# The byte offsets of the feed-forward input and activation made the same in all stages

## What is computed

```python
def half_ffn(x, shift, scale, gate, g, w_gu, w_down):
    h = modulate(x, g, shift, scale)
    a, u = jnp.split(h @ w_gu, 2, axis=-1)
    return x + FFN_RES * gate * ((jax.nn.silu(a) * u) @ w_down)
...
    for i in range(DEPTH):
        xp = half_ffn(xp, mp[0], mp[1], mp[2], norm_ff1[i], ff1_w_gu[i], ff1_w_down[i])
...
        xp = half_ffn(xp, mp[6], mp[7], mp[8], norm_ff2[i], ff2_w_gu[i], ff2_w_down[i])
```

## Time and profile before

| | |
|---|---|
| median of 3 runs | 3004.07 us (3003.33 to 3004.99) |
| the profiled execution | 3003.66 us, of it 3001.8 us span |
| TensorE busy | 98% |
| VectorE busy | 76% |
| ScalarE busy | 42% |
| mean granted TensorE clock | 0.998 |

### The profile page before, as it was taken

The page is one execution under the profiler, slowest core; times in us unless marked ns, Lnnn a source line. Parts: engine busy times, 40 slices in busy tenths (PEclk is TensorE's granted clock), DMA queues, the critical chain, the costliest instruction groups (busy, mean ns, idle before and its releaser), DMA issues.

```text
span 3001.8 us, 44338 instructions
## 1 busy us (share of the span) xinstructions
PE 2932.3 (98%) x17575; PEld 2838.0 (95%) x17575; DVE 2288.0 (76%) x3506; ACT 1247.5 (42%) x2001; POOL 127.7 (4%) x135
## 2 busy tenths in 40 slices
PE   8999989999999998999999999999999999999999
PEld 6999879999999988999999987799999999889999
DVE  6889887888787877778788877678878887667553
ACT  3332464433333355443333247644333323554432
POOL 0000110000000010000000011000000001320000
PEclk9999999999999999999999999999999999999999
DMA  7556304555455512455445521144555555315332
GB/s 285 201 213 224 122 32 173 185 195 208 168 189 194 200 67 72 189 189 206 185 180 192 210 101 57 58 179 186 208 191 189 189 213 180 106 59 182 126 134 97
DMA packets 87722, 490.21 MB, mean 163 GB/s; under 512 B 11825, under 2 KB 13169, under 8 KB 51377
## 3 DMA queue, kind: packets, MB, share of 16 engines
q1 hardware_dynamic: 83696, 480.42, 43.1%
q0 software_dynamic: 3904, 8.24, 1.1%
HBM read 485.33 MB, written 3.29 MB: 163 GB/s over the span
## 4 chain that ended last, share of the span: by engine, by line
PE 54%; issue 38%; DVE 4%; ACT 3%; DMA 1%; POOL 0%; SPq 0%; DVEq 0%; ACTq 0%; POOLq 0%
PE ps L753 16%; PE ps L773 8%; PE ps L758 8%; PE ps L794 6%; PE ps L949 4%; PE ps L777 4%; PE ps L737 1%; PE ps L893 1%; DMA boot<-in_mod_w 1%; PE ps L928 1%; PE ps L878 1%; PE ps L871 1%; PE ps L967 0%; PE ps L1022 0%; PE ps L841 0%
## 5 line engine op out<-in xcount | busy, mean ns | idle before, releaser
L753 PE MATMUL ps<-h_hi,w_hi 128*128 128x386 f32 x2688 | 911.0, 339 | 0.1
L753 PE MATMUL ps<-h_lo,w_hi 128*128 128x386 f32 x2688 | 907.2, 337 | 0.0
L1451 DVE TENSOR_TENSOR w_lo<-w_raw,w_hi 128x2048 fp32r<-128x2048 f32 (+3 forms) x282 | 705.8, 2503 | 40.4 <-ACT w_hi L1133 40.1
L1471 DVE CUSTOM_DVE_ANT_0 F_junk<-F_slab,cond,mod_b 128x1024 f32<-128x1024 f32 x544 | 706.5, 1299 | 12.7
L1133 ACT ACTIVATE w_hi<-w_raw 128x2048 fp32r<-128x2048 f32 (+4 forms) x278 | 578.8, 2082 | 18.0 <-DMA w_raw<-in_ffn_dn 12.2
L753 PEld LDWEIGHTS ps<-h_lo,w_hi 128*128 128x128 f32 x2688 | 506.8, 189 | 0.0
L753 PEld LDWEIGHTS ps<-h_hi,w_hi 128*128 128x128 f32 x2688 | 506.3, 188 | 0.4 <-ACT w_hi L1133 0.4
L758 PE MATMUL ps<-h_hi,w_lo 128*128 128x386 f32 x2688 | 501.5, 338 | 0.0
L758 PEld LDWEIGHTS ps<-h_hi,w_lo 128*128 128x128 f32 x2688 | 476.3, 189 | 0.0
L773 PE MATMUL ps<-F_act_hi,w_hi 128*128 128x384 f32 x1408 | 474.3, 337 | 0.0
L773 PE MATMUL ps<-F_act_lo,w_hi 128*128 128x384 f32 x1408 | 472.9, 336 | 0.0
(11 more groups left out here) (358 smaller groups left out, 3324.0 us busy)
## 6 DMA issues: line engine op xcount, KB each, us to landing
w_raw<-in_ffn_gu SPq DMA_DIRECT2D x176, 1024.0 KB, 4.8
F_slab<-in_mod_w SPq DMA_DIRECT2D x272, 512.0 KB, 5.6
w_raw<-in_ffn_dn SPq DMA_DIRECT2D x64, 1408.0 KB, 6.4
w_raw<-in_d_w SPq DMA_DIRECT2D x8, 1536.0 KB, 6.8
boot<-in_mod_w SPq DMA_DIRECT2D x8, 1024.0 KB, 10.2
w_raw<-in_a_w SPq DMA_DIRECT2D x4, 1536.0 KB, 6.3
w_raw<-in_b_w SPq DMA_DIRECT2D x4, 1536.0 KB, 6.3
w_raw<-in_c_w SPq DMA_DIRECT2D x8, 544.0 KB, 3.6
```

The source lines that it names most:

```text
L753: pe.matmul(ps[:, 2 * par + u, 0:N_MOVE], w[0][:, k, u, :], h[:, k, :], start=(k == 0 and h is h_hi), stop=False)
L1451: dve.tensor_tensor(w_lo[par][:, 0:w], w_raw[par][:, 0:w], w_hi[par][:, 0:w], ALU.subtract).then_inc(w_split_lo.sem, 1)
L1471: dve.tensor_tensor_reduce(out=junk[:], in0=w, in1=cond[:, c, :], scale=scale, scalar=mod_b[:, n:n + 1], op0=ALU.mult, op1=ALU.add, accum_ ...
```

## The change

All feed-forward stages get the offsets that the seventh had for its input, (24, 56) elements or 96 and 224 bytes, and the one that the third had for its activation, 40 elements or 160 bytes. All mixers get (0, 32), which mixer A had. The tables and the function `activation_of` go; the rooms keep their sizes. The instructions and their order on each engine, their waits and their transfers are the same as before.

```diff
--- before.py
+++ after.py
@@ -20,7 +20,6 @@
 TT = N_TOK // P
 N_MOVE = N_TOK + 2
 N_ROW = 448
-ROOM = 56
 N_PAST = 128
 D_FF = 2816
 KF = D_FF // P
@@ -91,9 +90,8 @@
     return "ABCD"[(s // 3) % 4] if s % 3 == 1 else "F"
 
 
-H_AT = [(8 * (s // 3 + 4 * (s % 3 == 2)), 8 * ((s // 3 + 4 * (s % 3 != 2)) % 8)) for s in range(N_STAGE)]
-ACT_ROOM = 120
-ACT_AT = {s: 2 * (8 + 16 * i,) for i, s in enumerate(t for t in range(N_STAGE) if t % 3 != 1)}
+ROOM_HI, ROOM_LO = 24, 56
+ACT_ROOM = 40
 
 
 def chunk_base():
@@ -260,7 +258,7 @@
 
 
         x = sb("x", [P, KD, N_TOK])
-        h_room = [sb(f"h_{what}", [P, KD * N_ROW + ROOM], F32R) for what in ("hi", "lo")]
+        h_room = [sb(f"h_{what}", [P, KD * N_ROW + ROOM_LO], F32R) for what in ("hi", "lo")]
 
         w_raw = [sb(f"w_raw{i}", [P, SLOT]) for i in range(2)]
         w_hi = [sb(f"w_hi{i}", [P, SLOT], F32R) for i in range(2)]
@@ -269,8 +267,9 @@
         def input_of(s):
 
 
-            return [z[:, at:at + KD * N_ROW].rearrange("p (k n) -> p k n", k=KD)[:, :, 0:N_MOVE]
-                    for z, at in zip(h_room, H_AT[s])]
+            at = (ROOM_HI, ROOM_LO) if s % 3 != 1 else (0, 32)
+            return [z[:, i:i + KD * N_ROW].rearrange("p (k n) -> p k n", k=KD)[:, :, 0:N_MOVE]
+                    for z, i in zip(h_room, at)]
 
         ident = sb("ident", [P, P])
         ones = sb("ones", [P, P])
@@ -426,7 +425,7 @@
                     with ExitStack() as at_first:
                         v["boot"] = [at_first.enter_context(nc.sbuf_tensor(f"boot{i}", [P, BOOT_COLS], F32))[:]
                                      for i in range(KD)]
-                    v["act"] = [part(f"act_{what}", [P, KF * N_TOK + ACT_ROOM], F32R) for what in ("hi", "lo")]
+                    v["act"] = [part(f"act_{what}", [P, KF * N_TOK + 120], F32R) for what in ("hi", "lo")]
                     v["slab"] = [part(f"slab{i}", [P, D]) for i in range(SLAB_SLOTS)]
                     v["junk"] = part("junk", [P, D])
                     continue
@@ -500,11 +499,7 @@
                         v["kout"] = part("kout", [P, 2 * HD])
                         v["bias"] = [part(f"bias{i}", [P, 2, 6, GRID_W]) for i in range(2)]
                         v["mask"] = part("mask", [P, GRID_W])
-        def activation_of(s):
-
-
-            return [z[:, at:at + KF * N_TOK] for z, at in zip(tiles["F"]["act"], ACT_AT[s])]
-
+        act_hi, act_lo = [z[:, ACT_ROOM:ACT_ROOM + KF * N_TOK] for z in tiles["F"]["act"]]
 
         def turned_out(kind, p):
 
@@ -760,7 +755,6 @@
                 mm.then_inc(w_used.sem, 1)
 
             def dn_step(s, m, par, first=False):
-                act_hi, act_lo = activation_of(s)
                 c = GU_STEPS + m
                 pe.wait_ge(w_split_hi.sem, w_split_hi.after(s, c))
                 pe.wait_ge(x_updated.sem, x_updated.at[s] + m - 1)
@@ -1178,7 +1172,6 @@
                                bias=z[:, N_TOK + 1:N_TOK + 2]).then_inc(silu_ready.sem, 1)
                 split_hi(CB[s] + j + 2 - par, par, w_next)
                 act.wait_ge(prod_ready.sem, prod_ready.after(s, j))
-                act_hi = activation_of(s)[0]
                 act.activation(act_hi[:, bass.ds(j * N_TOK, N_TOK)], tmp[par][:, 0:N_TOK],
                                ACT.Copy).then_inc(act_hi_ready.sem, 1)
 
```

## The result

The changed kernel takes 2979.0 us (median of 4 runs, 2977.5 to 2979.7) against 3004.5 us before (4 runs): ratio 0.9914, 95% interval 0.9897 to 0.9931. Forecast were 2978.0 us and a range of 2974.5 to 2986.5. The profiled execution has a span of 2976.7 us, 25.1 less than before.

A forecast was written before the change was run, and what follows sets the result against it. TensorE, busy for 98% of the span, was taken to bound the kernel. Gains of 21.54 (gate/up), 3.26 (down), 0.32 (step 0) and 1.0 (mixers) sum to 26.1 us: 3004.07 - 26.1 = 2978.0 us, range 2974.5 to 2986.5.

The forecast's parts named there:

- Gate/up: Steps 1 to 21 of all eight feed-forward stages: each takes the seventh's 174.94 us, gain 21.54 us.
- Down: Down steps of all eight feed-forward stages, activation at 40 elements: 735.82 us before, 732.56 after, gain 3.26 us.
- the bounds (91.57 and 91.36): Down part per stage: the seventh's 91.57 us (gain 3.26 us, taken) or the third's 91.36 (gain 4.94).
- Step 0: Gate/up step 0 with the statistics inside: all eight take the seventh's 9.49 us, gain 0.32 us, bounds 0 and 0.5.
- Mixers: Mixer input at (0, 32): D gains 1.0 us; B and C taken as 0, with 0.5 us either way.
- The stages do differ by the address: Rival denied here: the matmul doesn't care, stages differ for another reason, the change does nothing: 3004 us, 3%.
- the slow pattern: Stages staying at 8.52 us a gate/up step: one to three, 2982 to 2990 us, 8%; seven, both parts, 3017.8, 2%.
- VectorE in the first stage: Rival: VectorE becomes the bound in the first stage, whose gain of 4.6 us is lost: 2982.6 us, 3%.
- A fixed spacing: Skill page's view: N / 2.4 GHz plus about 2.5 ns a matmul, 163.3 ns for 386 columns; no address matters, sum 0.

The follow-up runs named there:

- the reordered step 0: Changed kernel with each feed-forward stage's step 0 doing all hi and lo products with w_hi first, then the 16 with w_lo: 2985.3 us (one run).
- the slow-places kernel: Same edit as the changed kernel, but all feed-forward inputs at (8, 40) and all activations at 8 elements: 3021.1 us, ratio 1.0055 against the kernel before.

## Why the prediction was right

**The sum.** 26.1 us were forecast, 25.1 measured in the profiled execution and 25.5 in the medians.

- *Gate/up, 21.5 forecast, 21.3 measured.* Right to 0.3 us, and by the mechanism forecast: the place of the operands. The missing part is the start of the first stage: its steps 1 and 2 take 8.70 and 8.45 us, against 8.52 and 8.34 in the others. It comes from its step 0, since with the reordered step 0 it took 174.74 us like the others.

```profile
47.91:56.61 8.70, 8.68 (x49) 1.00 0.87 341
56.61:65.06 8.45, 8.45 (x49) 1.00 0.54 190
```

- *Down, 3.3 forecast, 3.2 measured.* The choice between the bounds (91.57 and 91.36) was right, and for the reason given: the start depends on what ran ahead. With the activation alone at 40, the seventh stage took 91.57 behind the input that all have now, and five others 91.36 behind other inputs.
- *Step 0, 0.3 forecast, 0.6 measured*, a little over the upper bound of 0.5. I had taken the seventh's 9.49 for all, but that stage itself went to 9.38. The activation of the stage ahead did it: with the activation alone moved it took 9.37, with the input alone 9.49.
- *Mixers, 1.0 forecast, 0.0 measured.* This is where the sum was off. The step itself was right: the 60 matmuls of D took 10.53 us as in A.

```profile
2497.65:2508.18 10.53, 10.53 (x61) 1.00 0.66 163
```

By the end of its 576 matmuls on the rooms, D was 0.8 us ahead of the kernel before; with the activation alone changed, and the mixers' input left where it was, it was not ahead at all (149.73 us). The remaining part of D gave 0.5 us back. So the address was worth about what I had put down for it. What the sum lacked were two terms of other kinds. TensorE waits 1.0 us more for VectorE at the start of A (see VectorE below). And the stretches at half clock came to lie elsewhere: A got a second one, worth up to 1.7 us, and C lost both of its own and was 2.2 us shorter. That is not the change: the changed kernel, profiled again, had its stretches in A, C, C and D, and its mixers took 3.0 us more. That D's and B's gains, A's loss and C's gain add up to 0.0, and that the whole so came within 1.0 us of the forecast, is in part luck: the spread by some microseconds that these stretches make should have been a term of the range.

**The rivals.** The stages do differ by the address (the slow-places kernel). Nothing stayed in the slow pattern: every stage from the second on started with 8.52 and left it in the next step, the first started with 8.70 and left it one step later. The doubt was sound in kind, for the reordered step 0 shows that the same step has two rhythms; but all stages were entered alike, and so all left alike.

VectorE in the first stage came true in part. Within the stage TensorE never waited: VectorE's 159.2 us lie in 175.1, and its 84.8 in 91.6. But VectorE then had its work on the first stage and on A's first weights still to finish, and TensorE, which now arrives sooner, waited 1.3 us for its last sums of squares in place of 0.3. That gives back the first stage's gain of 1.1 us in its down part. It is this part that counts: the wait is there with the activation alone moved, and not with the input alone. Of the 4.6 us that I had put on this case 1.0 was lost. The cover in the other stages was also a little thinner than I wrote: in the second stage VectorE is busy for 143.5 of 174.94 us, 18% to spare and not over a fifth.

**A fixed spacing against the trace.** By the fixed spacing of "TensorE: Matmul & The Clock Gate", "Wait — 56ns, not 53.3ns?", in the Trainium skill nothing would have moved. The trace disagrees: here a matmul of 386 columns in a full stream took from 173.6 to 180.0 ns (stage averages), and the stationary operand's place counted as much as the moving one's. In "SBUF — State Buffer", the Trainium skill says that TensorE never waits on anyone in its part on the two sides of SBUF ("SBUF: two separate sides"), not in the one on a bandwidth pool that the prediction names.

## What to carry to other kernels

When a program repeats a block with operands at different places, its own trace is the survey: cut one window per repeat and compare. In this kernel, TensorE's time for a gate/up part moved by up to 3.7% (174.94 to 181.44 us) with the places of the operands, and the best place seen could be copied and came out to a hundredth of a microsecond in seven of eight stages. An added tensor that shifts the inputs against the weights can cost as much: 32 unused bytes ahead of the weights cost 33 us here, more than the 25.5 us that the change had brought.

And a gain on the engine that bounds the kernel can end in a wait for the next one: in the first stage, where VectorE has the most to do, 1.0 of the 4.3 us won went into a wait at the next stage's start.

## What the runs showed of the hardware that I had not expected

- The time of a full stream of matmuls goes by relations between addresses, as far as tried: all operands 32 bytes on, 174.94 us again; the weights alone 32 bytes on, 178.08 us, which is the value of inputs 32 bytes back.
- It has a memory: the same 16 matmuls took 2.78 or 2.88 us by what ran before them. In the changed kernel the slow start of a gate/up part is gone after two steps, and the slow start of a down part after one.
- Half-clock stretches of 3.4 or 6.8 us in the mixers come and go from run to run, between three and seven in the profiled ones. Mixer C took 202.3 us with none, 204.4 with 6.8 us of them in all and 208.3 with 17.1 us. In the profiled executions that, and not the feed-forward stages, makes most of the spread of this kernel's times.
- Why one distance is faster than another stays open. The runs show that it goes by the distance of the streams and their history; they don't show which part of the memory or of the engine makes it so.
